# Second block: output products by tile, norm and halves beside them, down products by tile

## The reference

```
h = rmsnorm(x, norm_mix[layer])
mix = attention branches of h            # layer 0: dilated attention and latent attention
                                         # layer 1: spatial gating and neighbourhood attention
x = x + mix @ w_out                      # output product, 1024 x 1024
h = rmsnorm(x, norm_ffn[layer])
gu = h @ ffn_w_gu                        # 1024 x 5632, gate and up
x = x + (silu(gate) * up) @ ffn_w_down   # 2816 x 1024
```

## Time and profile before

| | us |
|---|---|
| median of the runs | 1775.72 |
| the profiled execution | 1774.15 |
| its span, first to last instruction | 1772.1 |
| TensorE busy | 1515.9 (86%) |
| VectorE busy | 959.1 (54%) |
| ScalarE busy | 561.8 (32%) |
| mean granted TensorE clock | 0.953 of full |

### The profile page before, as it was taken

One profiled execution on the slowest core, in us unless ns is written; L12 is line 12 of the kernel. 1 busy time (PEld: TensorE's weight loads), 2 busy tenths in 40 slices (PEclk: granted clock), 3 DMA queues, 4 the chain that ended last, 5 costly groups with the idle time before them and its releaser, 6 DMA issues.

```text
span 1772.1 us, 18024 instructions
## 1 busy us (share of the span) xinstructions
PE 1515.9 (86%) x6822; PEld 1057.0 (60%) x6822; DVE 959.1 (54%) x1916; ACT 561.8 (32%) x1195; POOL 315.6 (18%) x296
## 2 busy tenths in 40 slices
PE   6999699879987777678988769986999969869997
PEld 5768587555533322233333227664999869559996
DVE  2896431375576677677766443233555454245554
ACT  1001530123333333433333224342333334333333
POOL 2000000033344444344445400400000000000000
PEclk9999899989999999899999989998999979989999
DMA  9964013299999999999999935313344523124551
GB/s 258 201 199 171 4 48 143 95 387 385 395 420 419 420 419 418 394 419 410 410 419 415 420 141 223 102 48 142 146 187 190 194 102 147 68 108 180 190 190 48
DMA packets 52022, 428.67 MB, mean 242 GB/s; under 512 B 6880, under 2 KB 7032, under 8 KB 9824
## 3 DMA queue, kind: packets, MB, share of 16 engines
q0 software_dynamic: 40720, 279.20, 40.8%
q1 hardware_dynamic: 11216, 148.33, 22.0%
HBM read 422.50 MB, written 4.98 MB: 241 GB/s over the span
## 4 chain that ended last, share of the span: by engine, by line
PE 66%; DMA 17%; DVE 9%; ACT 5%; issue 2%; POOL 1%; DVEq 0%; SPq 0%; ACTq 0%; POOLq 0%
PE psum L611 24%; DMA pool<-uv,experts 16%; PE psum L850 11%; PE psum L716 9%; PE psum L717 9%; PE psum L718 9%; DVE pool L1566 2%; PE psum L644 2%; PE psum L674 2%; DMA ring<-stream 1%; DVE w_lo L1328 1%; ACT xn L946 1%; ACT diag L1153 1%; POOL pool L568 1%; ACT L1143 1%
## 5 line engine op out<-in xcount | busy, mean ns | idle before, releaser
L850 PE MATMUL psum<-pool,diag 128*128 128x512 f32 x1024 | 487.7, 627 | 132.0 <-ACT diag L1153 122.0
L850 PEld LDWEIGHTS psum<-pool,diag 128*128 128x128 f32 x1024 | 196.1, 199 | 418.1 <-issue 210.9
L1566 DVE CUSTOM_DVE_ANT_0 pool<-pool,xn 128x1024 f32<-128x1024 f32 x256 | 313.8, 1226 | 207.5 <-DMA pool<-uv,experts 205.9
L568 POOL DMA_INDIRECT pool<-uv,experts x256 | 283.7, 1108 | 703.9 <-PE psum L850 359.0
L1328 DVE TENSOR_TENSOR w_lo<-ring,w_hi 128x2048 fp32r<-128x2048 f32 x76 | 173.9, 2292 | 182.7 <-ACT w_hi L1003 182.7
L1003 ACT ACTIVATE w_hi<-ring 128x2048 fp32r<-128x2048 f32 x76 | 145.0, 1911 | 284.7 <-PE psum L718 284.7
L716 PE MATMUL psum<-h_hi,w_hi 128*128 128x256 f32 x704 | 201.4, 286 | 22.4 <-DVE h_lo L1367 22.4
L717 PE MATMUL psum<-h_lo,w_hi 128*128 128x256 f32 x704 | 201.0, 286 | 0.0
L718 PE MATMUL psum<-h_hi,w_lo 128*128 128x256 f32 x704 | 200.9, 285 | 0.0
L611 PE MATMUL psum<-hT,ring 128*128 128x256 f32 x768 | 171.1, 385 | 5.5 <-DMA ring<-stream 2.9
L611 PEld LDWEIGHTS psum<-hT,ring 128*128 128x128 f32 x768 | 148.1, 193 | 28.8 <-issue 5.1
(11 more groups left out here) (234 smaller groups left out, 1774.3 us busy)
## 6 DMA issues: line engine op xcount, KB each, us to landing
ring<-stream SPq DMA_DIRECT2D x66, 2048.0 KB, 7.9
pool<-uv,experts POOLq DMA_INDIRECT x256, 12.5
ring<-stream SPq DMA_DIRECT2D x3, 1024.0 KB, 6.0
t_scratch<-att POOLq DMA_DIRECT2D x1, 2048.0 KB, 90.8
rpb_scratch<-att POOLq DMA_DIRECT2D x7, 256.0 KB, 28.2
ring<-stream SPq DMA_DIRECT2D x1, 1792.0 KB, 10.2
row<-rows POOLq DMA_DIRECT2D x1, 1672.0 KB, 15.4
ring<-stream SPq DMA_DIRECT2D x1, 1664.0 KB, 7.0
```

Of the source, the lines that this page charges most:

```text
L568: gp.indirect_dma_start(out=gath[:, n % NROWS, :], out_offset=None, in_=uv, in_offset=bass.IndirectOffsetOnAxis(ap=experts[:, n:n + 1], ax ...
L850: last = nc.tensor.matmul(psum[:, RB + half, :], diag[:, n % NDIAG, :], gath[:, n % NROWS, D + 512 * half:D + 512 * half + 512], start=k = ...
L1566: ins = V.tensor_tensor_reduce(out=row_u, in0=row_u, in1=xn[:, n // SLOTS, :], scale=1.0, scalar=0.0, op0=ALU.mult, op1=ALU.add, accum_out ...
```

## The change

It changes orders, not amounts of work; the matmuls, copies and loads are the same in number and shape.

- Output products (`mix_output`): the order becomes half 0 tile 0, half 1 tile 0, half 0 tile 1, transposes of tile 0, half 1 tile 1, transposes of tile 1. The list of fills follows.
- ScalarE's and VectorE's feed-forward begin with the adds, root, norm, gained copies and halves of tile 0, then a weight part, then those of tile 1, then the second part. The first part's split no longer waits for the last output product but for the transposes of the attention output; for this the buffer of a part is chosen by q % 2.
- Down products: tile is the outer loop in a part. The last two parts run interleaved: both for tile 0, then both for tile 1. The adds and norms follow by tile.
- Projections of layer 1: TensorE waits for tile 0's halves first and for tile 1's when it comes to them; VectorE makes tile 0's halves, part 0's low half, tile 1's halves, part 1's low half, and then clears the padding.

The core of the diff:

```diff
+def output_fills(name, norm):
+    out = [(name, 0, 0), (name, 1, 0), (name, 0, 1), (norm, 0, 0), (norm, 0, 1)]
+    return out + [(name, 1, 1), (norm, 1, 0), (norm, 1, 1)]
...
-            return tensor[:, PART_NO[layer, q] % 2, :].rearrange("p (k n) -> p k n", k=KD)
+            return tensor[:, q % 2, :].rearrange("p (k n) -> p k n", k=KD)
...
             def projections(layer):
-                pe.wait_ge(h_split, 4 * 2 * layer + 4)
...
                         for t in range(NT):
+                            if c == 0 and side == 0:
+                                pe.wait_ge(h_split, 4 * 2 * layer + 2 * t + 2)
...
+                product(0, 0)
+                product(1, 0)
+                product(0, 1)
+                tile_transposes(norm, 0, xn[:, 0, :])
+                product(1, 1)
+                tile_transposes(norm, 1, xn[:, 1, :])
...
+                for q in range(DOWN, LAYER_PARTS - 2):
+                    for t in range(NT):
+                        last = down_products(q, t)
+                    last.then_inc(part_read, 1)
+                for t in range(NT):
+                    last = down_products(LAYER_PARTS - 2, t)
+                    if t == NT - 1:
                         last.then_inc(part_read, 1)
+                    down_products(LAYER_PARTS - 1, t)
...
-                if q in (GU, GU + 1):
+                if q == GU:
+                    act.wait_ge(bank_filled, FILL_NO[(("attB", "attD")[layer], "OT", 0, NT - 1)] + 1)
+                elif q == GU + 1:
                     wait_part_output(layer)
...
-                split_high(layer, GU)
-                split_high(layer, GU + 1)
+                for t in range(NT):
+                    for i in range(2):
+                        wait_emptied(act, (("evout", "odout")[layer], i, t))
+                    root(x[:, t, :], xn[:, t, :], ssq[:, t:t + 1], t, D)
+                    split_high(layer, GU + t)
...
-                normed(name)
+                name, source = "ffn%d" % layer, ("evout", "odout")[layer]
+                add_part(source, 0, 0)
+                add_part(source, 1, 0)
+                normed_tile(name, 0)
+                add_part(source, 0, 1)
+                halves_tile(name, 0, h_hi, h_lo)
                 split_low(layer, GU)
+                add_part(source, 1, 1)
+                normed_tile(name, 1)
+                halves_tile(name, 1, h_hi, h_lo)
                 split_low(layer, GU + 1)
-                gained_halves(name, h_hi, h_lo)
...
-                add_to_x("down%d" % layer)
+                for t in range(NT):
+                    for n in range(2):
+                        add_part("down%d" % layer, n, t)
+                    if layer:
+                        normed_tile("F2", t, None, row[:, LATE["final2"][0]:LATE["final2"][1]], out_ready)
+                    else:
+                        normed_tile("mix1", t)
...
-            normed("mix1")
+            halves_tile("mix1", 0, p_hi, p_lo)
+            split_low(1, 0)
+            halves_tile("mix1", 1, p_hi, p_lo)
+            split_low(1, 1)
             clear_padding(kdz)
-            split_low(1, 0)
-            split_low(1, 1)
-            gained_halves("mix1", p_hi, p_lo)
```

More of the change, by code:

```diff
@@ L153, in fill_list @@
             out += tm_fills("vd") + [("gating", t) for t in range(NT)] + [("coutT", t) for t in range(NT)]
-            out += attention_fills("attD", HEADS2) + tm_fills("odout", 2)
-        out += norm_fills("ffn%d" % layer) + fm_fills("gu%d" % layer, KF // 2)
-        out += [("down%d" % layer, half, t) for half in range(2) for t in range(NT)]
+            out += attention_fills("attD", HEADS2) + output_fills("odout", "ffn1")
+        out += fm_fills("gu%d" % layer, KF // 2)
+        out += [("down%d" % layer, half, t) for t in range(NT) for half in range(2)]
     return out
@@ L751, in projections, with mix_output, product @@
                             last.then_inc(part_read, 1)
+            def mix_output(name, norm):
+                def product(i, t):
+                    w = wait_chunk(pe, (name, i))[:, 0:4096].rearrange("p (k n) -> p k n", k=KD)
+                    dst = begin((name, i, t))
+                    accumulate(dst, [(oT[:, k, tile128(t)], w[:, k, :]) for k in range(KD)]).then_inc(bank_filled, 1)
+                product(0, 0)
[4 more added lines that the diff above has]
+                tile_transposes(norm, 1, xn[:, 1, :])
             def feed_forward(layer):
-                norm_transposes("ffn%d" % layer, normed_rows)
                 pe.wait_ge(h_split, 4 * (2 * layer + 1) + 4)
@@ L757, in feed_forward, with down_products @@
                     split_feature_major(layer, q, (h_hi, h_lo))
-                banks = {(n, t): begin(("down%d" % layer, n, t)) for n in range(2) for t in range(NT)}
-                for q in range(DOWN, LAYER_PARTS):
+                banks = {(n, t): begin(("down%d" % layer, n, t)) for t in range(NT) for n in range(2)}
+                def down_products(q, t):
+                    w = [v.rearrange("p k n -> p (k n)") for v in wait_part(layer, q)]
                     j = q - DOWN
-                    w = [v.rearrange("p k n -> p (k n)") for v in wait_part(layer, q)]
                     pe.wait_ge(gu_ready, KF // 2 * layer + j + 1)
[L763 to L771, removed]
+                    for n in range(2):
+                        for k in (2 * j, 2 * j + 1):
+                            c = D * (k % 2) + 512 * n
+                            last = split_products(banks[n, t], [v[:, k, tile128(t)] for v in (gu_hi, gu_lo)],
+                                                  [v[:, c:c + 512] for v in w], k == 0, k == KF - 1)
+                        if k == KF - 1:
+                            last.then_inc(bank_filled, 1)
+                    return last
+                for q in range(DOWN, LAYER_PARTS - 2):
[5 more added lines that the diff above has]
+                    if t == NT - 1:
                         last.then_inc(part_read, 1)
+                    down_products(LAYER_PARTS - 1, t)
             pe.wait_ge(t5_landed, 48)
@@ L923, in _ @@
             wait_turned(attD)
[L924 removed]
+            mix_output("odout", "ffn1")
             feed_forward(1)
@@ L1250, in normed @@
[L1250 to L1264, removed]
+                    normed_tile(name, t, dst, rows_, signal)
@@ new lines, in normed_tile @@
+            def normed_tile(name, t, dst=None, rows_=None, signal=None):
+                dve.wait_ge(root_ready, roots_before[name] + t + 1)
+                r = rstd[:, t:t + 1]
+                link(V.reciprocal(r, r))
+                d = (xn if dst is None else dst)[:, t, :]
+                if rows_ is None:
+                    ins = V.tensor_scalar(d, x[:, t, :], r, None, ALU.mult)
+                else:
+                    ins = V.scalar_tensor_tensor(d, x[:, t, :], r, rows_, ALU.mult, ALU.mult)
+                ins.then_inc(xn_ready if signal is None else signal, 1)
@@ new lines, in gained, with gained_tile @@
+            def gained(name, dst):
+                for t in range(NT):
+                    gained_tile(name, t, dst)
+            def gained_tile(name, t, dst):
+                g = par_(gain_of[name]) if name in gain_of else None
+                for hf in range(2):
+                    b = wait_filled(dve, (name, t, hf)).rearrange("p (k n) -> p k n", k=4)
+                    d = dst[:, 4 * hf:4 * hf + 4, tile128(t)]
+                    if g is None:
+                        ins = V.tensor_copy(d, b)
+                    else:
+                        ins = V.tensor_tensor(d, b, g[:, 4 * hf:4 * hf + 4].unsqueeze(2).to_broadcast([P, 4, P]),
+                                              ALU.mult)
+                    ins.then_inc(emptied_sem((name, t, hf)), 1)
@@ L1266, in add_to_x, with add_part @@
+            def add_part(name, i, t):
+                b = wait_filled(dve, (name, i, t))
+                d = x[:, t, 512 * i:512 * i + 512]
+                V.tensor_tensor(d, d, b, ALU.add).then_inc(emptied_sem((name, i, t)), 1)
             def add_to_x(name):
@@ L1268, in add_to_x @@
                     for t in range(NT):
-                        b = wait_filled(dve, (name, i, t))
-                        d = x[:, t, 512 * i:512 * i + 512]
-                        V.tensor_tensor(d, d, b, ALU.add).then_inc(emptied_sem((name, i, t)), 1)
+                        add_part(name, i, t)
             def attention(a):
@@ L1359, in gained_halves, with halves_tile @@
             def gained_halves(name, high, low):
-                gained(name, hT)
                 for t in range(NT):
[L1363 to L1368, removed]
-            def feed_forward(layer):
-                name = "ffn%d" % layer
-                normed(name)
+                    halves_tile(name, t, high, low)
+            def halves_tile(name, t, high, low):
+                gained_tile(name, t, hT)
+                for hf in range(2):
```

(12 more changed lines are left out.)

21 lines of the change are left out of this document (5 added, 16 removed).

## The result

The changed kernel takes 1752.66 us (median of four runs, 1750.94 to 1756.68) against 1775.66 for the kernel before: ratio 0.988, 95% interval 0.9851 to 0.9909. In a second comparison, of five rounds, it was 1756.74 against 1775.54: 0.9895 (0.9881 to 0.9909). The forecast was 1753.6 with a range of 1748.5 to 1758.5. "The trace" of the changed kernel is this execution; the second comparison kept one of its own, with a span of 1751.0, which I call the second execution.

What follows compares the result with a forecast made beforehand. TensorE bounds 66% of the chain, so time is saved only where it stands still, at four joints. Savings of 6.9 + 6.9 + 8.2 + 0.1 = 22.1 us from 1775.7 gave 1753.6, range 1748.5 to 1758.5.

Steps and rivals of the forecast that it cites:

- Output joints: Last output product to gate-up, each layer: 15.62 us falls to 7.55, less 1.14 for transposes, saving 6.9.
- The ring: Load of gate-up chunk 1 is issued 6.9 us later behind product (0,1), yet lands in time: no cost.
- The stall: In the last two down parts, TensorE waits 1.6 us because part 42 cannot be split before part 40 is read.
- Down joint: Layer 0's down products to layer 1's projections: 9.25 us after the last matmul, 10.85 with the wait, against 19.10; saves 8.2.
- The memsets: Padding memsets, 2.1 us of the old chain before layer 1's projections, move behind part 1's low half and cost nothing.
- Tail: Last down matmul to end of final norm: 4.1 us, 5.7 with the wait, against 5.8; saves 0.1.
- The clock: TensorE's restarts after joints, at 1.2 GHz for 3.09, 3.99 and 5.88 us, half of it loss; kept unchanged, called the unknown.
- The clock stays up: Rival: TensorE keeps 2.4 GHz through both output joints, gaining 1.5 + 2.9 us, giving 1749.2; chance 0.15.
- Second table load: Rival: the second Sqrt in each output joint needs another table load, 1.28 us a layer, giving 1756.2; chance 0.06.
- Missed cover: Rival: tile 0's 5.6 us of VectorE work falls after the last output product in both layers, giving 1764.8; chance 0.06.
- Moved idle time: Rival: TensorE starts sooner after joints but then waits as long for splits or chunks, giving 1775.7; chance 0.02.
- Slower down matmuls: Rival: new inner order slows 528 down matmuls from 0.227 us; 0.27 loses all 22 us, 0.433 gives about 1860; chance 0.03.

Runs made afterwards that it cites:

- the kernel with the output side alone: Changed kernel with down products and the step to layer 1 in the old order; 1760.44 us, 0.9905 of the kernel before.
- the down-only kernel: Changed kernel with output products and their norm and halves back in the old order; 1765.05 us, 0.9925 of the kernel before.
- the late split: Changed kernel with the high half of the first gate-up part waiting for the last output product again; 1764.35 us, 0.993 of the kernel before.
- the busy joints: Changed kernel with unread f32 products on constants while TensorE waits in three joints; 1749.11 us, with a third buffer pair too 1741.41 us.
- the kernel with third buffers: Changed kernel with the last down part split into a third buffer pair, waiting for no earlier part; 1750.38 us, 0.9851 of the kernel before.

## Why the prediction was right

It forecast 22.1 less; the medians show 23.0 less in the first comparison and 18.8 less in the second, and both times, 1752.66 and 1756.74, lie within its range. That the first lies within 1 us of the forecast is in part luck, since two executions of the changed kernel alone differ by 3.5. The mechanism is borne out term by term:

**Output joints.** 7.55 was worked out for the path of tile 1, 7.48 to 7.49 was measured wherever the clock held through the transposes (layer 1 here, both layers in the kernel with the output side alone). Small errors cancel in it: the hand-over to TensorE is 0.04, not 0.35, as the down-only kernel shows too, while the first four transposes take 0.67 and the copies 1.29, which were put at 0.60 and 1.20. Layer 0 lost another 0.7, which the prediction did not have: the clock fell with tile 1's transposes (granted 0.50 from 1221 on), and the chain took 1.98 for all eight and 0.69 for the last copy, against 0.67 for the first four and 1.29 for both copies in layer 1. The transposes in the product stream were put at 1.14; in the chain they are 0.87. The early split and the order of the queues did what was said: the late split costs 4.2 a layer, both steps of it. The ring cost nothing, as forecast: the next high half, at 1234.05, is released by TensorE's reading of a part and not by a load.

**The stall.** The mechanism and its place were right, the size was off: 1.6 of waiting was forecast and 2.0 a layer measured. The waiting itself is 1.67; most of the rest, 0.27, is TensorE's slow first matmul after a wait, which the prediction left out.

**Down joint.** 9.25 forecast, 9.05 measured, of which 0.25 is the hand-over, priced at 0.40. The memsets, now at 1431.24, cost nothing.

**Tail.** 4.1 after the last matmul (E') was forecast, 3.93 measured; with the stall of 2.0 this is 5.9 against 5.8 before, so the gain is nothing, where 0.1 was forecast.

**The clock.** The sum kept the loss at the restarts of the earlier trace rows. From the first matmul to the first spacing at full pace they are 3.2, 4.1 and 6.2 us in the kernel before and 5.2, 3.1 and 4.2 in the changed one, so with half of such a stretch as loss the three together lose 0.5 less; in its second execution they are 3.7, 5.6 and 6.3. The span from the output products to the end was 559.9 in the one and 563.4 in the other, and 1.6 of these 3.5 us is the restarts, another 1.6 layer 1's output products, which started at half clock in the second (22.43 for three products, 20.84 in the first), as they had in the earlier trace rows (29.27 against 27.72 in the earlier trace rows). That last, 1.5, is a gain of the profiled execution that no term of the sum had, and more than all it has above the forecast (23.2 against 22.1). The clock was named as the unknown; it is.

**The rivals.** *The clock stays up*: it fell in all three joints, in every kernel that left them idle. What would have kept it is shown by the busy joints, and its price too: the kernel with third buffers gets another 8 us faster (0.9851 to 0.9807, on one chip) once its three joints are busy. The prediction had put 4.4 on two of them, and 2.0 on the restart of the third. *Second table load*: none. ScalarE of the changed kernel in order of time:

```profile
1204.92 1.28 ACT L976 ACT_TABLE_LOAD   x1
1206.21 0.29 ACT L976 ACTIVATE small<-small 128x1 f32<-128x1 f32 x1
1206.41 1.89 ACT L1034 ACTIVATE w_hi<-ring 128x2048 fp32r<-128x2048 f32 x1
1218.36 1.06 ACT L975 ACTIVATE xn<-x 128x1024 f32<-128x1024 f32 x1 [10.05 <-DVE x L1308]
1219.32 0.19 ACT L975 ACTIVATION_READ_ACCUMULATOR xn<-x 128x1 f32 x1
1219.54 0.29 ACT L976 ACTIVATE small<-small 128x1 f32<-128x1 f32 x1
```

The second Sqrt, at 1219.54, follows Copy and Square without a load. For the Copy this agrees with the Trainium skill (ScalarE: Activation LUTs, "Table sets: the hidden batching unit"), which has copies in every table set. Its 2.66 us for a switch (the same page, "What ACT_TABLE_LOAD costs") did not show: the one load of the joint, at 1204.92, is again 1.28 and Sqrt starts 0.01 after it. *Missed cover*: not here; the late split shows that it would have come by the add that is queued behind. *Moved idle time*: the stage from gate-up to the end of the down products takes 186.85 without stall and half clock; 188.20 in the kernel before, less half of its 3.2 at half clock, is 186.6. *Slower down matmuls*: the same two numbers refute it; six matmuls running into one bank pace like three. The high halves of the changed kernel's last down parts start 5.44 apart (the last at 1404.00, the one before at 1398.56), the length of a part before.

## What to carry to other kernels

When a stage ends in a chain of one engine at a time and its data comes in independent tiles, ask which tile can be complete first, order the products for it, and lay its chain beside the other tile's last product; then read from the trace how much cover is left (here 2.3 us between tile 0's norm and its transposes, and 1.5 us before the last add), since in an engine's fixed order one late instruction takes everything behind it along. Interleaving parts to finish a tile sooner asks for more buffers at once: count who must be ready half a step earlier. And a joint that is left to one tile's chain still idles TensorE: filling it with products that nobody reads gave 8 us here, where the whole change gave 19 to 23. Filling it with real work only pays if this work costs no more than it replaces.

## What the runs showed of the hardware

In joints of 7.5 to 19 us in which TensorE did only transposes the granted clock fell to 0.50 (1.2 GHz) every time. With f32 products beside the transposes TensorE was busy for 6.2 of 7.4 us and 8.0 of 9.0 us, and the clock stayed at 1.00 (2.4 GHz) every time, in six joints of two kernels. After a drop the restart ran slow for 3.1 to 6.3 us, differently in executions of the same kernel: of the 3.5 us between two executions of the changed kernel, 1.6 is this. A matmul after a wait of 1.67 us took 0.50 on the chain instead of 0.23, with the granted clock at 1.00 through the wait. Split-operand matmuls with 128 columns moving start 0.11 us apart, with 256 columns 0.12.
